# Expert results of a mixture-of-experts layer by way of HBM rows, fetched per token, instead of a scatter on TensorE

## The reference

```python
def moe_swiglu(h, router_w, wg, wu, wd):
    logits = jnp.einsum('bsd,de->bse', h, router_w).astype(jnp.float32)
    top_val, top_idx = lax.top_k(logits, TOP_K)
    gates = jax.nn.softmax(top_val, axis=-1)
    combine = jnp.sum(jax.nn.one_hot(top_idx, N_EXPERTS, dtype=jnp.float32) * gates[..., None], axis=-2)
    out = jnp.zeros_like(h)
    for e in range(N_EXPERTS):
        out = out + combine[..., e:e + 1].astype(h.dtype) * swiglu(h, wg[e], wu[e], wd[e])
    return out
```

## Time and profile before

| | us |
|---|---|
| median of 3 runs | 1516.62 |
| lowest and highest | 1515.53, 1518.11 |
| the profiled execution's own time | 1514.14 |
| its span in the profile | 1512.0 |
| TensorE, VectorE, ScalarE, GpSimd busy | 98%, 78%, 65%, 3% |

### The profile page before, as it was taken

How to read it: one execution, slowest core, us unless ns; L and a number is a source line. 1 busy time by engine, 2 the same in 40 slices (tenths; PEclk the granted TensorE clock), 3 DMA queues, 4 the chain that set the end, 5 groups by cost and what they waited for, 6 DMA issues and landing times.

```text
span 1512.0 us, 19204 instructions
## 1 busy us (share of the span) xinstructions
PE 1487.2 (98%) x7301; PEld 1237.0 (82%) x7304; DVE 1175.3 (78%) x844; ACT 981.7 (65%) x757; POOL 48.9 (3%) x53
## 2 busy tenths in 40 slices
PE   9999999999999999999999999999999999999997
PEld 7987788888988878888878888887888888888885
DVE  5875544444787698898878888878889888888886
ACT  6574533444556677777777777776777777777774
POOL 1010000000000000002000000200000200000010
PEclk9999999999999999999999999999999999999999
DMA  9625555554552499999989999999999998999992
GB/s 348 217 72 181 188 180 188 193 177 129 195 167 98 148 327 382 375 357 372 372 305 360 373 374 350 376 329 336 373 368 363 366 375 320 363 371 376 350 374 108
DMA packets 190647, 437.71 MB, mean 289 GB/s; under 512 B 9376, under 2 KB 13664, under 8 KB 190448
## 3 DMA queue, kind: packets, MB, share of 16 engines
q1 hardware_dynamic: 188256, 433.91, 80.0%
q0 software_dynamic: 1120, 2.20, 0.6%
q10 hardware_dynamic: 1200, 0.56, 0.1%
HBM read 435.59 MB, written 1.05 MB: 289 GB/s over the span
## 4 chain that ended last, share of the span: by engine, by line
PE 95%; DVE 3%; ACT 1%; issue 1%; DMA 0%; ACTq 0%; SPq 0%; DVEq 0%
PE ps L1316 29%; PE ps L1318 29%; PE ps L1317 29%; PE ps L1611 2%; PE ps L1568 1%; PE ps L1586 1%; PE ps L1587 0%; PE ps L1813 0%; PE ps L1379 0%; PE ps L1378 0%; PE ps L1377 0%; PE ps L1371 0%; DVE w_lo L831 0%; DMA x<-in_x_dram 0%; DVE hm L821 0%
## 5 line engine op out<-in xcount | busy, mean ns | idle before, releaser
L1163 DVE TENSOR_TENSOR w_lo<-raw,w_hi 128x2048 fp32r<-128x2048 f32 x333 | 754.6, 2289 | 122.5 <-ACT w_hi L658 120.0
L658 ACT ACTIVATE w_hi<-raw 128x2048 fp32r<-128x2048 f32 x332 | 630.2, 1919 | 170.5 <-PE ps L1318 170.5
L1316 PE MATMUL ps<-w_hi,aT_hi 128*128 128x512 f32 (+1 forms) x1296 | 511.0, 394 | 8.3 <-issue 3.2
L1318 PE MATMUL ps<-w_hi,aT_lo 128*128 128x512 f32 (+1 forms) x1296 | 503.4, 388 | 0.0
L1317 PE MATMUL ps<-w_lo,aT_hi 128*128 128x512 f32 (+1 forms) x1296 | 502.5, 388 | 0.0
L1316 PEld LDWEIGHTS ps<-w_hi,aT_hi 128*128 128x128 f32 x1296 | 243.4, 188 | 61.8 <-issue 5.9
L1318 PEld LDWEIGHTS ps<-w_hi,aT_lo 128*128 128x128 f32 x1296 | 243.2, 188 | 51.8
L1317 PEld LDWEIGHTS ps<-w_lo,aT_hi 128*128 128x128 f32 x1296 | 243.6, 188 | 48.6
L831 DVE TENSOR_TENSOR w_lo<-raw,w_hi 128x2048 fp32r<-128x2048 f32 (+2 forms) x81 | 176.7, 2186 | 101.8 <-ACT w_hi L478 101.6
L478 ACT ACTIVATE w_hi<-raw 128x2048 fp32r<-128x2048 f32 (+2 forms) x81 | 148.2, 1830 | 106.8 <-PE ps L1318 105.7
L1316 PE MATMUL ps<-w_hi,s2T_hi 128*128 128x512 f32 x544 | 213.1, 392 | 0.0
(11 more groups left out here) (274 smaller groups left out, 910.9 us busy)
## 6 DMA issues: line engine op xcount, KB each, us to landing
raw<-in_moe_w_gate_dram SPq DMA_DIRECT2D x112, 1024.0 KB, 6.9
raw<-in_moe_w_up_dram SPq DMA_DIRECT2D x112, 1024.0 KB, 7.6
raw<-in_moe_w_down_dram SPq DMA_DIRECT2D x112, 1024.0 KB, 7.0
raw<-in_w_in_dram SPq DMA_DIRECT2D x20, 1024.0 KB, 7.1
raw<-in_ffn_w_gate_dram SPq DMA_DIRECT2D x14, 1024.0 KB, 5.1
raw<-in_ffn_w_up_dram SPq DMA_DIRECT2D x14, 1024.0 KB, 5.1
raw<-in_ffn_w_down_dram SPq DMA_DIRECT2D x14, 1024.0 KB, 4.9
raw<-in_w_out_dram SPq DMA_DIRECT2D x8, 1024.0 KB, 5.1
```

The costliest lines, as they stand in the source:

```text
L658: nc.scalar.activation(moe_hi(pos), raw[:, slot, :], ACT.Copy).then_inc(hi_ready, 1)
L1163: V.tensor_tensor(moe_lo(pos), raw[:, pos % 6, :], moe_hi(pos).bitcast(F32), ALU.subtract)\
L1316: mm(out, lhs_hi, rhs_hi, start=start, stop=False, skip_group_check=True)
L1318: return mm(out, lhs_lo, rhs_hi, start=False, stop=stop, skip_group_check=True)
```

## The change

In pairs 0 to 2 y is no longer scattered. ScalarE copies it from PSUM into an on-chip buffer (`y_rows`, in room that was used in the router alone) and issues a DMA of 512 KB that stores it in `expert_rows`, a scratch tensor in HBM with a block of 128 rows for each expert. At the start of the last pair GpSimd issues four indirect DMAs (first and second choice, two token blocks), each of which fetches one row of 4 KB per token by an index (`row_idx`, made in `list_rows` in the router) into `fetched`, and VectorE adds the four to x with the tokens' gates in chunks 2 to 5 of the last pair. Tokens whose expert is one of the last three (5, 6, 7) point to a block that holds zeros; these experts are scattered on TensorE as before, in the last pair. The blocks of `expert_rows` are zeroed by 15 stores of 512 KB from GpSimd's queue at the end of the first mixer. The transposes of `sel` are made only where `selT` is still needed: at the head of the last pair and at its end. The dummy y is stored too, so that `zero_y` is left out.

```diff
@@ GpSimd
                     pool.memset(xbc[:, :, 0:TAPS - 1], 0.0).then_inc(pad_set, 1)
+                    pool.memset(qkr[:, 0:D], 0.0).then_inc(zero_row_set, 1)
+                    pool.wait_ge(zero_row_set, 1)
+                    for n in range(2 * E - 1):
+                        pool.dma_start(expert_rows[n], qkr[:, 0:D]).then_inc(rows_zeroed, 16)
...
             with pool.Fori(0, last) as p:
                 build_sel(p + 1, 3)
+
+            pool.wait_ge(rows_stored, 32 * last)
+            pool.wait_ge(gath_psum, 8 * last + 8)
+            nc.gpsimd.tensor_tensor(small[:, 0, 9:10], zeros[:, 0:1], zeros[:, 0:1], ALU.mult)
+            pool.wait_ge(rows_listed, 1)
+            for i in range(2):
+                for b in range(NB):
+                    pool.indirect_dma_start(fetched[:, i, b, :], None, all_rows,
+                                            bass.IndirectOffsetOnAxis(row_idx[:, NB * i + b:NB * i + b + 1], axis=0))\
+                        .then_inc(rows_fetched, 16)
             build_sel(last + 1, 1)
@@ ScalarE, pair
-                def take_y():
-                    nc.scalar.activation(y_hi[:], banks(3, 5), ACT.Copy).then_inc(y_hi_ready, 1)
+                def take_y(k):
+                    act.wait_ge(split_used, g0 + 6 * k - 2)
+                    if more:
+                        nc.scalar.activation(y_rows[k // FC], banks(3, 5), ACT.Copy).then_inc(y_taken, 1)
+                    else:
+                        nc.scalar.activation(y_hi[:], banks(3, 5), ACT.Copy).then_inc(y_hi_ready, 1)
+
+                def store_y(k):
+
+                    act.wait_ge(y_taken, 2 * p + (k // FC + 1))
+                    act.dma_start(expert_rows[2 * p + k // FC], y_rows[k // FC]).then_inc(rows_stored, 16)
+
+                def y_stored(k):
+
+                    act.wait_ge(rows_stored, 32 * p + 16 * (k // FC + 1))
...
                     sp_(6 * k + 1)
+                    if more and k in (1, FC + 1):
+                        store_y(k)
                     sp_(6 * k + 2)
                     evac_sT(k)
+                    if more and k in (FC - 1, PAIR - 1):
+                        y_stored(k - FC + 2)
...
                     gather_lo(p + 1, 3)
-                    sel_transposed(p + 1)
@@ VectorE, router
                 split(MOE_BASE + 2, 2)
+                list_rows()
                 gates()
@@ VectorE, pair
+            def add_rows(j):
+
+                dve.wait_ge(rows_fetched, 16 * 2 * NB)
+                if j == 0:
+                    dve.wait_ge(x_added, 2)
+                else:
+                    dve.wait_ge(rows_added, j)
+                b, gate = j % NB, (sm(7), sm(6))[j // NB]
+                V.scalar_tensor_tensor(x[:, b, :], fetched[:, j // NB, b, :], gate[:, b:b + 1],
+                                       x[:, b, :], ALU.mult, ALU.add).then_inc(rows_added, 1)
...
-                    if k in (1, FC + 1):
-                        take_y_lo(2 * p + k // FC)
+                    if not more and k in (1, FC + 1):
+                        take_y_lo(k // FC)
...
+                    if not more:
+                        add_block(1, k)
+                        if 2 <= k < 2 + 2 * NB:
+                            add_rows(k - 2)
                     if more or k < PAIR - 1:
                         lo(6 * k + 5)
@@ TensorE, pair
-                    if k in (1, FC + 1):
-                        scatter(2 * p + k // FC, 0, k // FC)
+                    if not more and k in (1, FC + 1):
+                        scatter(k // FC, 0, k // FC)
                     transpose_s(k)
                     proj(1, e, 6 * k, 0)
                     proj(1, e, 6 * k + 1, 1)
-                    if k in (1, FC + 1):
-                        scatter(2 * p + k // FC, 1, k // FC)
+                    if not more and k in (1, FC + 1):
+                        scatter(k // FC, 1, k // FC)
 
                 for k in range(1, PAIR):
-                    if k == 1:
-                        pe.wait_ge(selT_ready, p + 1)
+                    if not more and k == 1:
+                        pe.wait_ge(gath_lo, p * 4 + 3)
+                        transpose_sel(range(2))
                     gate_up(k, k // FC)
                     pe.wait_ge(sT_lo, s0 + k)
+                    if more and k in (1, FC + 1):
+                        pe.wait_ge(y_taken, 2 * p + (k // FC + 1))
...
-                        for fill in range(6, 9):
+                        for fill in range(6, 8):
                             gather_fill(p + 1, fill)
@@ TensorE, start of the expert part (gather_first, moe)
-                pe.wait_ge(gath_lo, 2)
-                for i in range(2):
-                    for b in range(NB):
-                        ins = nc.tensor.transpose(ps[:, 7, (2 * i + b) * P:(2 * i + b + 1) * P],
-                                                  sel[:, b, i, :].bitcast(F32), ident)
-                ins.then_inc(gath_psum, 1)
...
                 last = pe.value_load(n_items[0:1, 1:2], min_val=E // 2 - 1, max_val=E - 1)
-                zero_y()
```

More of the change, by code:

```diff
@@ L745, in moe @@
                 pair(last, False)
-                norm(4, [x_added] * NB, (last * 4 + 5, last * 4 + 6))
+                norm(4, [x_added] * NB, (5, 6))
             def dense():
@@ L1104, in count, with list_rows @@
                 V.tensor_tensor(sm(6, 2), sm(6, 2), sm(1)[:, 2:4], ALU.mult).then_inc(gate_diff, 1)
+            def list_rows():
+                rank, expert, high = sm(9, 4), sm(9)[:, 4:8], sm(9)[:, 8:12]
+                limit = sm(9)[:, 12:13]
+                i4 = lambda a: a.rearrange("p (i b) -> p i b", i=2)
+                V.tensor_copy(i4(expert), top_idx[:, :, 0:2].rearrange("p b i -> p i b"))
+                V.tensor_scalar(limit, sm(14, 1), float(P), float(P * (E - 2)), ALU.mult, ALU.add)
+                chain(V.tensor_tensor(small[:, 4:6, :], small[:, 12:14, :],
+                                      bc(sm(15).unsqueeze(1), [P, 2, NB * E]), ALU.mult))
+                chain(V.tensor_reduce(rank, small[:, 4:6, :].rearrange("p i (b e) -> p (i b) e", b=NB), AX.X, ALU.add))
+                chain(V.tensor_scalar(high, rank, float(P), float(P * (E - 1)), ALU.is_gt, ALU.mult))
+                chain(V.scalar_tensor_tensor(rank, rank, float(P - 1), high, ALU.add, ALU.add))
+                chain(V.scalar_tensor_tensor(rank, expert, float(P), rank, ALU.mult, ALU.add))
+                chain(V.tensor_scalar(high, rank, limit, float(2 * P * E), ALU.is_ge, ALU.mult))
+                chain(V.tensor_tensor(rank, rank, high, ALU.add))
+                V.tensor_scalar(row_idx[:, 0:4], rank, float(P * (2 * E - 2)), None, ALU.min).then_inc(rows_listed, 1)
             def gates():
@@ L1120, in router @@
             def router():
-                V.memset(sel[:, :, 0, :].bitcast(F32), 0.0)
                 dve.wait_ge(rw_in, 16)
@@ L1203, in pair @@
                     gate_times_up(k)
-                    add_block1(k)
+                    if not more:
+                        add_block(1, k)
+                        if 2 <= k < 2 + 2 * NB:
+                            add_rows(k - 2)
                     if more or k < PAIR - 1:
@@ L1207, in pair @@
                     if k == FC + 3:
-                        dve.wait_ge(x_added, p * 4 + 4)
+                        dve.wait_ge(sel_built, p + 1)
+                        if not more:
+                            dve.wait_ge(x_added, 4)
                         select(p + 1, True)
@@ L1549, in mixer, with transpose_sel @@
                     w_out(1, 1, (1,))
+            def transpose_sel(picks):
+                for i in picks:
+                    for b in range(NB):
+                        ins = nc.tensor.transpose(ps[:, 7, (2 * i + b) * P:(2 * i + b + 1) * P],
+                                                  sel[:, b, i, :].bitcast(F32), ident)
+                ins.then_inc(selT_psum, 1)
             def gather_fill(p, fill):
@@ L1690, in pair @@
                     pe.wait_ge(sel_built, p + 2)
-                    for i in range(1):
-                        for b in range(NB):
-                            ins = nc.tensor.transpose(ps[:, 7, b * P:(b + 1) * P], sel[:, b, 0, :].bitcast(F32), ident)
-                    ins.then_inc(gath_psum, 9)
+                    transpose_sel(range(1))
                     pe.wait_ge(sT_lo, s0 + k)
@@ L1713, in zero @@
                 return ins
-            def zero_y():
-                zero((3, 4)).then_inc(y_zero, 1)
             def gather_first():
```

78 lines of the change are left out of this document (40 added, 38 removed).

## The result

The changed kernel takes 1502.69 us (median of 5 runs, 1501.95 to 1504.23) against 1516.62 us (5 runs, 1514.19 to 1518.11): ratio 0.9909, 95% interval 0.9898 to 0.9921, 13.9 us less. Forecast were 1503.1 us. The profiled execution took 1502.69 us with a span of 1500.9 us. Run again later, it gave 0.9911 (0.9895 to 0.9928).

A forecast was written before the change was run, and what follows sets the result against it. TensorE, busy 98%, was taken to bound the kernel, with transfers hidden in the weight stream's lead. Savings of 10.9 + 1.3 - 0.4 + 0.9 + 0.8 = 13.5 us gave 1516.62 - 13.5 = 1503.1 us, range 1500.8 to 1508.5.

The forecast's parts named there:

- 0.228 us per matmul: Expert part: TensorE is the pace, and each wide matmul removed saves its spacing in the chain, 0.228 us.
- 44 matmuls: Scatter in pairs 0 to 2 disappears for n = 0 to 5: 48 wide matmuls in all, 10.9 us.
- twelve transposes less four: Transposes of `sel` leave the gathers of three pairs, 1.3 us, and return once heading the last pair, -0.4 us.
- Start of the expert part: Before the first projection, transposes and `zero_y` go but a register load is exposed: 0.9 us, bounds 0.6 and 1.2.
- `y_lo` wait: At 537 us the weight load of scatter n = 0 waited for `y_lo`; this goes, 0.8 us.
- four adds: Last pair: four VectorE passes of 1.3 us, one per chunk, fit in some 2 us free per chunk.
- The sum: Whole kernel: 10.9 + 1.3 - 0.4 + 0.9 + 0.8 = 13.5 us less.
- First rival: After 537 us or around the fetch, transfers overrun the weights' lead; 1504.5 to 1511 us, middle 1507; chance 0.18.
- Second rival: Expert part: the average 358 GB/s is the memory's ceiling, so transfers become the bound; 1521 us; chance 0.04.
- Third rival: Last pair: indirect loads land late and VectorE waits; 1514 us if 60 us after 1253; chance 0.05.
- plain price: Fetch: indirect loads priced as plain 512 KB ones, issue 0.54 us, landing 4.7 us, 19 us for four in turn.
- The zero stores: Between 115 and 130 us, fifteen GpSimd stores, 7.9 MB, 21 us of transfer, stay hidden; uncovered up to 21 us.

The follow-up runs named there:

- 2: Changed kernel with eight unread matmuls of scatter's shape run again on TensorE at each of the six places: 1513.70 us.
- kernel 3: Kernel before, all matmuls kept, with VectorE's `y_lo` subtraction and adds of pairs 0 to 2 cut to 8 columns: 1514.93 us.
- Kernel 5: Changed kernel with three more stores of 1 MB of idle data beside each of its six 512 KB stores: 1511.28 us.
- kernels 6 and 7: Changed kernel with experts 5 and 6 also by HBM rows, only expert 7 scattered: 1500.02 us; then with the adds a chunk earlier: 1498.71 us.
- kernel 1: Changed kernel without zero stores, row stores, fetch and VectorE's four adds: 1503.56 us.

## Why the prediction was right

**TensorE is the bound, 0.228 us per matmul: shown** by 2 (matmuls back, time back) and 3 (VectorE relieved, hardly anything). From the first transposes of pair 0 to those of the last pair the kernel before took 738.55 us, the changed one 727.16: 11.4 us less. Predicted for this stretch were 44 matmuls (10.0 us), twelve transposes less four (0.9): 10.9. Of the remaining 0.5 us 0.4 is the gap at the loop's two jumps back (from one weight load to the next), 2.29 and 2.19 us before, 2.16 and 1.90 after. That difference was in no term. Over all traces here the two gaps together are 3.9 to 4.5 us in the nine kernels or runs with the change, 4.5 and 5.1 in the two without it (before, and kernel 3). So it may belong to the change; the cause is open.

**Start of the expert part, 0.9 us, and the `y_lo` wait, 0.8: right in size, the first for another reason.** From the gather's first matmul to the first projection it was 5.89 us and is 5.17, 0.7 less; from there to the first transposes 18.85 and 17.25, 1.6 less, which is the wait and the four matmuls of the first block (0.9). The chain in that place, to be laid beside the earlier trace rows: the four transposes and the zeroing are gone, and the projection follows `aT_lo` after 0.07 us. The prediction held back 0.3 of the 1.2 us for a register load that would come into the open. What came into the open is ScalarE's last copy, `aT_lo`, for which TensorE now waits 0.27 us; before, the transposes of `sel` stood beside it. And 0.2 us of the start is clock: the first half of the gather took 2.76 us where it took 2.59, at a granted clock of 0.53 (514 to 518 us; before 0.65 from 512 to 516). From the gather's second half to the projection it is 0.86 us less.

```profile
...
518.05 1.58 ACT aT_hi L660 x3
519.62 1.48 ACT aT_lo L660 x3
521.10 0.07 issue
521.18 0.47 PE ps L1388
...
```

**From the last pair's first transposes to the end: no change**, 235.3 us in both, as predicted with four adds put in.

**The sum** by the trace is 11.4 + 0.7 + 1.6 = 13.7 us, 13.5 in the forecast. By the medians it is 13.9, with an interval of 12.0 to 15.5; that forecast and median lie 0.4 us apart is closer than the measurement can tell, and so in part luck. The spans differ by only 11.1, because the profiled execution of the changed kernel arrived at the gather 2.6 us later (515.98 us, before 513.41). The lag is there before the change has done anything: GpSimd's first load of the norm row, before, ran 1.8 us later.

```profile
...
L418 POOL DMA_DIRECT2D bqk<-in_norm_w_dram x2: 533/540/547, 89.5 to 458.0; - x2
...
```

In the window from 40 to 90 us TensorE's granted clock was 0.97 where it was 1.00, and in the router (508 to 514 us, before 506 to 512) 0.75 against 0.95. The change is not the cause: kernel 3, which is the kernel before with less work for VectorE, shows 0.97 and 0.72 in the same two places. The forecast was made on the median and not on the profiled execution, which was 2.5 us better than its median. That choice was right: otherwise 1500.6 us would have stood there.

**First rival, part goes back to DMA: not here, but its mechanism exists.** The lead is about 5 us in the steady part. After the start of the loop it fell to 1.8 us (544 to 570 us, where it was 4.1 or more before) and was back by 620; behind the store at 653 us it fell to 3.3, behind that at 896 us to 1.7, behind the fetch from 9.4 to 3.3, and TensorE never waited for it. The text set a demand of 4.9 us against a lead of 3 to 5; some 3 were used at the start, while the engines moved 392 GB/s. Kernel 5 shows the end of the room: at 3.7 MB per place the first place costs 3.5 us.

**Second rival, the average rate as ceiling: falls.** 368 GB/s came over 954 us, 384 over 963 in kernel 5. The Trainium skill (DMA: Bandwidth & Descriptors, section Bandwidth) names about 358 GB/s as the limit of the HBM side, but says in the same section that each core gets roughly this when both cores of an HBM domain stream, and gives 425 GB/s as measured for 16 MB with the other core idle. This kernel runs on one core, and its 368 and 384 GB/s lie between the two: the prediction had taken up the first figure alone. The level at which the transfers are the limit shows in kernel 5, where splits wait for weights: 393 GB/s from 560 to 600 us, 402 from 650 to 700.

**Third rival, late fetch: falls.** One indirect load is dearer than the plain price taken (issue up to 5.5 times, landing up to 2.2), but the four overlap: from the first issue at 1243.4 to the last landing are 17 us, where 19 were taken for four plain ones in turn. In kernels 6 and 7 there were only 28 and 11 us from the last issue to the first add, and still no wait. How it shares the engines with the weights shows in the changed kernel's DMA queues from 1252 to 1258 us (q0 is GpSimd's, q1 SyncE's):

```profile
...
q0 software_dynamic: 308, 1.13, 51.4%
q1 hardware_dynamic: 319, 1.14, 49.5%
...
```

The Trainium skill's rule that each DMA engine takes turns between its queues (DMA: Bandwidth & Descriptors, section SWDGE vs HWDGE vs iDMA) agrees: 308 packets to 319, and half the bytes each, as the prediction said. Half the bytes hold only because these packets are of one size (3.6 KB); in kernel 5 the turns are as even and the bytes are nearly 4 to 1.

**The zero stores** raise 115 to 130 us from 207 to 305 GB/s at a DMA share of 0.85; kernel 1, which has none, gains nothing.

## What to carry to other kernels

Where one engine's queue is 98% busy and its feeders wait for it, price a removed instruction by its spacing in the chain, not by its row's duration (0.228 us here, 0.39 in the row): the sum comes out within a few per cent. Bytes that come in bursts cost nothing until a burst exceeds the lead of the loads, so compare each burst with the lead at its place (here between 1.7 and 10 us, low after the start of the part and behind a burst), and ask how large the burst's packets are beside those of the loads; an average share of 100% says little. Work on an engine with spare time still hurts where it stands in front of the last pieces before a drain; put it a chunk earlier (0.6 us here).

## What was not expected of the hardware

**The clock fell to half behind a gap.** At each of its two jumps back the expert loop leaves 1.9 to 2.6 us between two weight loads of TensorE, where 0.23 is the rule. At 20 of the 22 jumps in the eleven traces the clock stays up. In the second run of the changed kernel the gap at 773.3 us was 2.47 us, and soon after it matmuls came 0.43 us apart in place of 0.23, eight in a row, at 1.2 GHz:

```profile
...
773.50 0.40 PE L1390 MATMUL ps<-w_hi,s2T_lo 128*128 128x512 f32 x1
775.74 0.49 PE L1388 MATMUL ps<-w_hi,aT_hi 128*128 128x512 f32 x1 [1.84 <-issue]
776.07 0.39 PE L1389 MATMUL ps<-w_lo,aT_hi 128*128 128x512 f32 x1
...
777.02 0.63 PE L1390 MATMUL ps<-w_hi,aT_lo 128*128 128x512 f32 x1
777.45 0.63 PE L1388 MATMUL ps<-w_hi,aT_hi 128*128 128x512 f32 x1
777.88 0.63 PE L1389 MATMUL ps<-w_lo,aT_hi 128*128 128x512 f32 x1
...
```

The window from 776 to 780 us has a granted clock of 0.62, the one before it 1.00, and this jump costs 2.0 us more than the next one: 0.4 of it the longer gap, 1.6 the clock. In kernel 3's profiled execution (its slowest, 1518.29 us) the same followed a gap of 2.53 us, but not one of 2.56 in the pair before; the gaps of up to 2.29 us had no such sequel in any trace here. So the length of the gap alone does not decide it. Such falls may be part of the spread of 3 to 5 us between runs: in every group the slower executions tend to have the lower mean clock (kernel 5: 1508.56 us at 0.996, 1514.94 at 0.992). Where in the execution it fell is known for the profiled ones alone.
